# RWKV scan of a two-layer backbone: another order for the pieces of preparation, inverse and chain within a slot

## What is computed

```python
def rwkv_scan(scan_in, S0, with_out):
    def step(S, inp):
        w_t, k_t, v_t, a_t, b_t = inp[:5]
        sa = jnp.einsum('dbhij,dbhj->dbhi', S, a_t)
        S = S * w_t[..., None, :] + sa[..., :, None] * b_t[..., None, :] + v_t[..., :, None] * k_t[..., None, :]
        return S, (jnp.einsum('dbhij,dbhj->dbhi', S, inp[5]) if with_out else None)
...
    S_c, y_c = rwkv_scan(in_c, S0, with_ctx_out)
    _, y_x = rwkv_scan(in_x, S_c, True)
    out_x = rwkv_out(y_x, *aux_x, r_k, ln_w, ln_b, w_out)
```

## Time and profile before

| | |
|---|---|
| median of 3 timed runs | 2489.04 us (2487.47 to 2489.66) |
| span of the profiled execution, first to last instruction | 2492.5 us |
| PE matmul busy | 2305.1 us, 92% of the span |
| DVE, ACT, POOL busy | 1104.5, 914.2, 660.4 us |
| mean granted TensorE clock | 0.979 of full speed |

### The profile page before, as it was taken

The page is one execution under the profiler, slowest core; times in us unless marked ns, Lnnn a source line. Parts: engine busy times, 40 slices in busy tenths (PEclk is TensorE's granted clock), DMA queues, the critical chain, the costliest instruction groups (busy, mean ns, idle before and its releaser), DMA issues.

```text
span 2492.5 us, 65234 instructions
## 1 busy us (share of the span) xinstructions
PE 2305.1 (92%) x27583; PEld 1906.5 (76%) x27583; DVE 1104.5 (44%) x2425; ACT 914.2 (37%) x1627; POOL 660.4 (26%) x481
## 2 busy tenths in 40 slices
PE   5998899899999999999988888888888889999998
PEld 4776677788888888878847777777776768888887
DVE  4326666351121112463356666666666645411213
ACT  4655555352121213452224334334243223422324
POOL 0334555312332332213311211111111110344442
PEclk8999999999999999999999999999999999999999
DMA  8125555112111221123410000000000011323321
GB/s 250 51 52 161 177 170 170 52 51 68 64 59 62 67 68 51 52 76 119 140 46 24 20 12 18 12 15 23 12 15 23 4 53 52 101 86 101 101 94 59
DMA packets 172316, 176.37 MB, mean 71 GB/s; under 512 B 26512, under 2 KB 160032, under 8 KB 172064
## 3 DMA queue, kind: packets, MB, share of 16 engines
q1 hardware_dynamic: 171200, 169.48, 21.7%
q10 hardware_dynamic: 864, 3.15, 0.3%
HBM read 161.06 MB, written 11.53 MB: 69 GB/s over the span
## 4 chain that ended last, share of the span: by engine, by line
PE 83%; DVE 7%; issue 5%; ACT 3%; SPq 1%; DMA 1%; POOL 1%; ACTq 0%; DVEq 0%
PE PS L398 38%; PE PS L1479 5%; PE PS L560 4%; PE PS L418 3%; PE PS L1464 2%; PE PS L757 2%; PE PS L738 2%; PE PS L1618 2%; PE PS L1454 2%; PE PS L1291 2%; PE PS L717 2%; PE PS L1563 1%; PE PS L747 1%; PE PS L1224 1%; PE PS L1593 1%
## 5 line engine op out<-in xcount | busy, mean ns | idle before, releaser
L378 POOL TENSOR_TENSOR WL<-RAW,WH 128x1024 fp32r<-128x1024 f32 x160 | 383.6, 2419 | 947.9 <-ACT WH L359 947.9
L398 PE MATMUL PS<-AH,WH 128*128 128x256 f32 (+1 forms) x992 | 350.8, 354 | 3.3 <-DVE AL L2355 2.4
L398 PE MATMUL PS<-AH,WL 128*128 128x256 f32 (+1 forms) x992 | 351.7, 355 | 0.0
L398 PE MATMUL PS<-AL,WH 128*128 128x256 f32 (+1 forms) x992 | 349.1, 352 | 0.0
L359 ACT ACTIVATE WH<-RAW 128x1024 fp32r<-128x1024 f32 x160 | 159.9, 1047 | 273.4 <-PE PS L398 265.7
L398 PE MATMUL PS<-BH,WL 128*128 128x512 f32 (+1 forms) x672 | 239.2, 356 | 0.0
L398 PE MATMUL PS<-BH,WH 128*128 128x512 f32 (+1 forms) x672 | 238.5, 355 | 0.0
L398 PE MATMUL PS<-BL,WH 128*128 128x512 f32 (+1 forms) x672 | 237.6, 354 | 0.0
L398 PEld LDWEIGHTS PS<-AH,WH 128*128 128x128 f32 x992 | 187.7, 189 | 31.4 <-issue 2.6
L398 PEld LDWEIGHTS PS<-AL,WH 128*128 128x128 f32 x992 | 187.0, 189 | 27.3
L398 PEld LDWEIGHTS PS<-AH,WL 128*128 128x128 f32 x992 | 187.4, 189 | 25.3
(11 more groups left out here) (276 smaller groups left out, 5027.4 us busy)
## 6 DMA issues: line engine op xcount, KB each, us to landing
ADW<-l_ada_w SPq DMA_DIRECT2D x40, 1024.0 KB, 5.4
RAW<-l_mlp_up SPq DMA_DIRECT2D x64, 512.0 KB, 4.5
RAW<-l_mlp_down SPq DMA_DIRECT2D x64, 512.0 KB, 4.0
RAW<-l_w_rkv SPq DMA_DIRECT2D x24, 512.0 KB, 5.2
rwkv_scratch<-STG SPq DMA_DIRECT2D x24, 384.0 KB, 3.4
ADA<-l_ada_w SPq DMA_DIRECT2D x4, 2048.0 KB, 11.6
RAW<-l_w_in SPq DMA_DIRECT2D x16, 256.0 KB, 5.2
RAW<-l_w_out SPq DMA_DIRECT2D x16, 256.0 KB, 5.2
```

Source lines behind the costliest of these rows:

```text
L378: e.tensor_tensor(WL[:, s, rows], RAW[:, s, rows], WH[:, s, rows], ALU.subtract).then_inc(w_split[h], 1)
L398: mm = e.matmul(dst, w[:, s, k, n * P:(n + 1) * P], r[:, k, lo:hi], start=(k == 0 and i == 0), stop=(k == KT - 1 and i == 2), skip_group_c ...
```

## The change

Only the two strings are replaced. Each has the same number of letters of each kind as before (33 p, 40 i, 41 c), so that every engine issues the same operations with the same waits, in another order.

```diff
-        SLOT = (("ipciciiciippcipcpcipicicicpiciciccicpccicicpipcicpicpicpicip"
+        SLOT = (("ipcicipicpcpiicpcpcicipcipiccicpcpcpcipcicipicpiciicpcicippc"
```

More of the change, by code:

```diff
@@ L1187, in build @@
         HALVES = (slice(0, 64), slice(64, 128))
-        SLOT = (("ipciciiciippcipcpcipicicicpiciciccicpccicicpipcicpicpicpicip"
-             "icipcpicpicpicpicpppicicpipcppicipipcipciipppccciccpci"),
-                ("cciicpciicpicipcpicpciicicppipcippcicipcpicicicipcpicipcicic"
-             "ppcicpicicpcicppipcicipcicpicpicppicicpcpcpicipiipipci"))
+        SLOT = (("ipcicipicpcpiicpcpcicipcipiccicpcpcpcipcicipicpiciicpcicippc"
+                 "picicipciipcpicpipcipicpicpipciipciippiciicpiicccppccc"),
+                ("cciicpcpicpcciiipcpcicipcipcppipcicpiciicicpicicpcipicipcici"
+                 "cppcicpicpciicppicicicppicpicpiipcpiccicipipccppipipic"))
         def slots(e, pre, inverse, chain):
```

## The result

The kernel with the new strings takes 2531.36 us (median of 4, 2529.91 to 2533.66), the one before 2489.21 us in the same comparison (4 runs, 2487.47 to 2489.66). The ratio is 1.0172, with a 95% interval of 1.0159 to 1.0184. The forecast had the right sign and was half the size: +42 us measured, +20 forecast, and 2531 lies above the range of 2474 to 2526.

A forecast was written before the change was run, and what follows sets the result against it. It took TensorE to be held by chain steps, VectorE/ScalarE order and, where dense, instruction supply. Terms summed to +2.9 us a pair, +20 us over seven pairs, so 2509 us; range 2474 to 2526 for 8 in 10.

The forecast's parts named there:

- The step that failed: Slots 16 and 17, the last of the scan: taken as unchanged, with 2 us to either side.
- even c1 to c15: Even slot, first stretch: VectorE holds for the key rates and later chain operations stand behind it, +1.0 us a pair.
- even c20 to c25: Even slot: fewer records and one large VectorE operation instead of five, 5.3 us against 6.30, -1.0 us a pair.
- odd c1 to c25: Odd slot: two steps without matmuls between cost 0.3 us each, a gain and a loss of 1.0 follow; together +0.3 us.
- the seam: Odd slot from c39 to the next c1: the wait moves from i37 to p0, the copy's time is saved, -0.4 us.
- The chain of the key rates: Even slot before c15: first table load hidden, rates ready at 12.95 us after c1, VectorE's key operation ends at 13.96.
- the walk of the old order: Hand count of the old even slot from c1 to c15: 15.8 us, where the trace has 15.98.
- The dense stretches: c25 to c35, more matmul records in both slots: +1.7 us in the even one, +1.0 in the odd one.
- the instruction floor: Where pieces are dense, TensorE gets a block of about 246 records no sooner than every 4.0 us.
- The rival on the other side: Instruction supply does not bind c25 to c35: -2 us a pair, 2475 us, shown by windows under 13.5 and 11; chance 0.26.
- I leave this cost where it is: p0 after the odd slot's end: stays at the lower clock, 2.35 us instead of 1.60, since the idle time is as long.
- a second dip of the clock: Even slot between p8 and i11: gaps bring the lower clock, +8 us more, 2517; chance 0.20 with other dearer cases.

The follow-up runs named there:

- e3: The changed kernel with one added wait: GpSimd's subtractions for the weights after the scan held until the last chain is done; 2506.09 us, ratio 1.0076.
- e4: The kernel before with one added wait: GpSimd's subtractions held until the last chain is done, as a control; 2487.73 us, ratio 1.0001.
- e5: The kernel before with GpSimd's subtractions held until TensorE's c3 of slot 17, so that they run beside L1713; 2512.91 us, ratio 1.0091.
- e1: The kernel before with the new strings in slots 0 to 15 only, the old ones in slots 16 and 17; 2499.76 us, ratio 1.0043.
- e2: The kernel before with the new strings in slots 16 and 17 only, the old ones in slots 0 to 15; 2515.06 us, ratio 1.0096.
- e9: The kernel before with one already-met wait and an empty instruction added behind each step of an odd inverse piece; 2565.8 us, one execution.
- e10: The kernel before with two already-met waits, each with an empty instruction, added behind each step of an odd inverse piece; 2778.0 us, one execution.
- e6: The kernel before with the new even string in slots 0 to 14 and GpSimd's subtractions held until after the scan; 2499.65 us, ratio 1.0046.
- e8: The kernel before with two bare empty instructions behind each step of an odd inverse piece, which the compiler dropped; 2486.66 us.
- e11: The kernel before with the new even string, its key-making piece moved behind c13, and GpSimd's subtractions held until after the scan; 2495.91 us, ratio 1.0034.
- e7: The kernel before with the new odd string in slots 1 to 15 and GpSimd's subtractions held until after the scan; 2496.42 us, ratio 1.0029.

## Why the prediction was right in sign and short in size

**The step that failed** is "slot 16 no preparation and slot 17 only the chain; I take them as unchanged, with 2 us to either side". They were worth 28.8 us of 37.9. The right sign came from the full slots. That the total was only twice the forecast is in part luck: the full slots gave about half of their +20, and the term put at nothing gave more than all of it. I took a slot whose pieces keep their order for one that keeps its time. Its order was unchanged on each engine, but what ran beside it wasn't: when ScalarE's copies L1667 for the weights end, and with them GpSimd's start, depends on where the end of the even string leaves ScalarE against TensorE. That moved by 0.4 us (GpSimd started 0.28 us behind c1 before, 0.15 us ahead of it after), and L1713, which came 0.3 us before GpSimd's second operation, came 0.1 us behind its start. e3 and e4 show that the collision is the cause of the 25 us, e5 that it is enough by itself in most executions. The earlier trace rows were misread as well: between the two chain pieces of that step TensorE runs a matmul of L1563 (0.70 us), so it wasn't waiting for VectorE only. It is this matmul that makes a lower clock dear in slot 17: 35 steps at 1.57 us instead of 0.89 are 24 us more.

**Slot 16** (+3.5 us): e1, e2 and e3 (37.7, 41.3, 42.1) show that its new string costs 3 us, with the lower clock granted for 20.5 us there instead of 10.2 in the records. Why it is granted longer was not tested; the new string begins with several chain pieces that have few matmuls of the inverse between them.

**The full slots**, where the whole prediction stood, came out at +7.9 us for seven pairs between the two profiled executions (+10.4 from the mean of five with the old strings to the mean of three with the new) where I had +20. Mean of seven slots, in us:

| stretch | before | after | difference | forecast |
|---|---|---|---|---|
| even c1 to c15 | 16.18 | 16.82 | +0.6 | +1.0 |
| even c15 to c20 | 5.94 | 6.49 | +0.5 | +0.7 |
| even c20 to c25 | 6.62 | 5.05 | -1.6 | -1.0 |
| even c25 to c35 | 14.49 | 16.08 | +1.6 | +1.7 |
| odd c1 to c25 | 27.52 | 27.03 | -0.5 | +0.3 |
| odd c25 to c35 | 12.10 | 13.39 | +1.3 | +1.0 |
| odd c35 to c39 | 4.97 | 4.99 | 0.0 | -0.4 |
| odd c39 to even c1 | 7.43 | 6.54 | -0.9 | -0.4 |

Four of the eight terms are within 0.4 us, the others within 0.8. The sum of the differences is +1.1 instead of +2.9 a pair, since the errors lean the same way: six of the eight terms came out below their forecast, odd c1 to c25, even c20 to c25 and the seam by most (0.8, 0.6 and 0.5 us). From the mean of the five executions to that of the three the same terms are +0.7, +0.6, -1.7, +1.7, -0.3, +1.1, 0.0 and -0.6, +1.5 a pair: the even c20 to c25 and the odd c1 to c25 stay too large by 0.7 and 0.6 us, and the seam comes within 0.2.

*Even c1 to c15.* The chain of the key rates is as it was told. Timeline after, slot 8:

```profile
1631.54 1.28 ACT L1210 ACT_TABLE_LOAD   x1
...
1633.31 0.96 DVE L1378 TENSOR_SCALAR TB<-PS 128x768 f32<-128x768 f32 x1 [1.00 <-PE PS L1247]
1634.30 0.84 ACT L1210 ACTIVATE TB<-TB 128x768 f32<-128x768 f32 x1 [1.48 <-DVE TB L1378]
...
1635.16 1.28 ACT L1212 ACT_TABLE_LOAD   x1
...
1636.46 0.94 ACT L1212 ACTIVATE TB<-TB,EPSC 128x768 f32<-128x768 f32 x1
...
1637.43 1.02 DVE L1383 SCALAR_TENSOR_TENSOR KK<-KG,PAR,TB 128x768 f32<-128x768 f32 x1 [0.62 <-ACT TB L1212]
...
1638.85 0.27 PE L1604 MATMUL PS<-AR,SS 64*64 64x64 f32 x2 [1.31 <-DVE RH L1710]
```

The first load is hidden (1.48 us of idle time lie between it and its activation), L1383 waits 0.62 us for the rates, and TensorE 1.31 us for the chain's operation behind it. From c1 (1624.56) the keys end at 13.9, where I had 13.96. TensorE reaches c15 at 16.68, and at 16.82 in the mean of seven slots, where I had 16.85. The term was 0.4 too large on the other side: the walk of the old order gave 15.8 and its mean is 16.2. The lower clock is in the measured terms here, too. With the new strings (after, e1, e3) it was granted between c11 and c20 in 12 of 21 even slots, which take 23.7 us from c1 to c20 where the other nine take 22.8; so about 0.5 of the +1.3 us a pair is the clock, and the waits gave about 0.8 of the 1.7 forecast for the two stretches.

*The dense stretches.* Both grew by what the instruction floor gave, +1.6 and +1.3. (In the odd one 724 + 96 = 820 records are 13.3 us by the floor and not 13.1, so that its term should have been +1.2.) Of slot 4 after, two gaps in its stretch c25 to c35, and the windows from one gap to the next:

```profile
1464.54 0.34 PE L1623 MATMUL PS<-MT,VSA 128*64 128x64 f32 x4 [1.26 <-issue]
...
1468.53 0.21 PE L1464 MATMUL PS<-XIT,AR 64*64 64x64 f32 x1 [1.28 <-issue]
```

```profile
1464.48:1468.54 4.06, 2.72 (x125) 2.51 (x125) 2.34 (x6) 0.45 (x2) 0.73 (x1) 1.00 0.02 4
1468.54:1472.90 4.36, 3.61 (x127) 3.34 (x126) 3.10 (x7) 0.89 (x4) 0.73 (x1) 1.00 0.01 4
```

250 and 253 records, 4.06 and 4.36 us: the spacing and count of the earlier trace rows again, with gaps of 1.3 us where they were 0.5 to 1.1. The traces tie these gaps to the instruction blocks. This is the DMA rate in 40 slices of 0.51 us in the window 1646.9 to 1667.3 of the kernel before, in which nothing but the five blocks is moved:

```profile
GB/s 0 0 0 32 0 0 0 0 0 0 0 0 32 0 0 0 0 0 0 0 32 0 0 0 0 0 0 0 32 0 0 0 0 0 0 0 32 0 0 0
```

The transfers start at 1653.3, 1657.3 and 1661.5, and the gaps of the earlier trace rows end at 1655.89, 1660.10 and 1663.90, 2.4 to 2.8 us behind. It is so throughout: between 1340 and 2000 us there are 28 gaps of 0.2 us or more in the middle of a group of matmuls of one line before and 35 after, and each of the 63 ends 2.1 to 3.0 us behind the start of a block's transfer, though the blocks come 5.2 to 5.3 us apart in the mean. In the even stretch c25 to c35 such gaps add up to 0.8 us a slot before and 1.8 after, in the odd one to 0.7 and 1.8, which is the larger part of both terms. That the gaps are waits for these blocks is thus well supported, and e9 and e10 fit it, but no run forced it. The rival on the other side (under 13.5 and 11 us) is out. So is the guess that the floor is exact: 18 of the 123 spacings between blocks between 1340 and 1990 us of the kernel before are under 4.0 us, the shortest 3.3; and slot 8 after, 15.31 us for 1020 records, is 1.3 us under the floor, while the mean of seven slots is 0.2 under the 16.3 of the forecast.

*Odd c1 to c25.* The walk had -1.0 for c15 to c20 and gave +1.0 back behind p14; measured were -1.3 and +1.1, and c1 to c15, where I had +0.3, was -0.3.

*The seam.* Timeline after, end of slot 9:

```profile
1714.81 0.41 PE L1464 MATMUL PS<-XIT,AR 64*64 64x64 f32 x16
...
1716.17 0.63 ACT L1687 ACTIVATE YQ<-YQ 128x512 f32<-128x512 f32 x1
1716.71 0.79 ACT L1360 ACTIVATE LV<-PS 128x768 f32<-128x768 f32 x1
...
1717.64 1.64 PE L1224 MATMUL PS<-W2X,LW 128*128 128x128 f32 x12 [1.95 <-ACT LV L1360]
```

The gap of 1.95 us is where the prediction put it, ahead of L1224, and as long as before. But p0 takes 1.64 us and not the 2.35 of the earlier trace rows: the lower clock isn't granted there, and between these two executions 0.5 us more a pair is saved than forecast. "I leave this cost where it is" was wrong for them. Of the six p0 of the even slots 4 to 14, five take over 2 us in the kernel before and one in the kernel after. Over more profiles the difference is smaller: with the old odd string (before, e2, e4, e5, e6, e8, e11) 22 of 42, from five of six in the kernel before to one of six in e11; with the new one (after, e1, e3, e7) 7 of 24. So the kernel before was caught in an execution with many dips, the gain at the seam is nearer 0.6 us than 0.9, and whether the same gap brings the lower clock less often when it stands ahead of p0 is not shown.

The rival *a second dip of the clock* came true in part where it was placed, and at full price elsewhere. In the kernel after, the lower level comes at c13 of slots 2, 10 and 12 for 3.4 or 6.8 us (before: once, at c15 of slot 12); in e11, with the same even string but for the keys, in all seven even slots. The seam has fewer dips in exchange, and over slots 2 to 15 the lower level is granted for 24 us in both profiled executions. The expensive one came in slot 17, for 54.6 us. I had priced a dip by the ones that the trace of before showed, and none there lasted beyond 10.2 us in the scan.

## What to carry to other kernels

After a reordering, look past the reordered loop: what the neighbouring phase has in flight at the seam shifts by tenths of a microsecond, and where TensorE is full beside a dependent chain, a fall of its clock is paid whole. Prefetch work on GpSimd that reads SBUF should be given a place by a wait of its own rather than run whenever its input lands, when VectorE has SBUF to SBUF operations in a chain there; in the old order this costs nothing (e4) and it takes the largest risk away. Before a granted clock is counted as a fixed cost, price one case in which it falls once and doesn't come back for the rest of a stretch (here 36.3 us at 2.4 GHz, 60 to 62 at 1.2).

## What the runs showed of the hardware

A VectorE operation of 0.24 us, SBUF to SBUF, that starts while GpSimd's SBUF operation is running ends 0.05 us behind that operation's end, whatever is left of it: 0.38 us (before), 2.26 (after and e2), 2.30 and then 0.42 (e5). VectorE's operations that read PSUM beside it keep their 0.22 to 0.29 us.

TensorE's granted clock isn't a function of the program alone. After 1.4 us of idle time in slot 17 it fell and stayed at 1.2 GHz for 54.6 us in the kernel after (51.2 in e2), over the same alternation of chain pieces and L1563 that runs at 2.4 GHz in the kernel before; in e10 it fell ahead of slot 17, without such a wait in it, and stayed at 1.2 GHz for 61.4 us. After the same idle time in e5 it stayed up in the profiled one of five executions. What decides is open. A collision that costs 1.5 us can so cost 25.

Gaps of TensorE in the middle of a group of its matmuls go with the transfers of its instruction blocks: all 63 of 0.2 us or more in the scans of before and after end 2.1 to 3.0 us behind the start of one.
